# Turning the activations of two gated feed-forwards on VectorE instead of TensorE, in an fp32 two-layer block kernel

## The chip, the core and the metric

The kernel runs on one core of a Trainium2 chip, as one launch. The metric is the device time of the whole launch in microseconds (us), lower is better. Names of engines in the rows: PE is TensorE's matmuls, PEld its weight loads, DVE is VectorE, ACT is ScalarE, POOL is GpSimd, SP is SyncE, which here only issues DMAs.

## The reference, cut to what matters

Two transformer blocks over 256 tokens of width 1024, in fp32. The first has differential attention, retention and a squared-ReLU feed-forward; the second has, around its attention, two gated feed-forwards of hidden width 2816, with separate weights. These two are what the change touches:

```python
def swiglu(x, w_gate, w_up, w_down):
    return (jax.nn.silu(x @ w_gate) * (x @ w_up)) @ w_down
...
x = x + FFN_RES * swiglu(rms_norm_2(x, ffn1_norm[l]), ffn1_w_gate[l], ffn1_w_up[l], ffn1_w_down[l])
...
x = x + FFN_RES * swiglu(rms_norm_2(x, ffn2_norm[l]), ffn2_w_gate[l], ffn2_w_up[l], ffn2_w_down[l])
```

`w_gate` and `w_up` are 1024 x 2816, `w_down` is 2816 x 1024.

## The kernel before, in words

Every fp32 product is made of three products of a reduced type, fp32r: both operands are split into a high part (rounded) and a low part (what is left), and high x high, high x low and low x high are added up in PSUM. So each weight is streamed from HBM once, in **units** of 128 x 2048 (1 MB), in program order. For each unit SyncE issues the load into `raw`, one of 6 buffers; ScalarE writes the high part (`hi(u)`, line 1128, into `w_hi`, one of 4 buffers); VectorE writes the low part in place (`lo(u)`, line 1570, `w_lo<-raw,w_hi`); TensorE then uses both (`products`, line 523). `hi(u)` waits until TensorE has used unit u-4, the load until it has used unit u-6.

Activations need the same split, and must in addition lie with the contracted dimension on the partitions. A gated feed-forward (called a stage here: `f1` and `f2` in the names) is worked in 11 **blocks** of 256 hidden columns. For a block i:

- TensorE multiplies the normed tokens (`hA`) by the gate and up columns, two units of K, for two halves of 128 tokens each (`tb` 0 and 1): 2 x 2 x 4 x 3 = 48 matmuls of 128 x 512 (`ff_up`).
- ScalarE takes SiLU of the gate half (`silu`, line 1389, `act_r`), VectorE multiplies it by the up half (`multiply`, line 1906, `act_f<-bank,rs,act_r`). `act_f` has the tokens on the partitions.
- TensorE turns `act_f` with four 128 x 128 transposes (`ff_turn`, line 537, `bank<-masks,act_f`; `masks` holds the identity), two into each of the PSUM banks 6 and 7. ScalarE writes their high part (line 1135, `fT_hi<-bank`), VectorE the low part (line 1589, `fT_lo<-bank,fT_hi`), each in two instructions.
- TensorE multiplies `fT` by the block's 256 rows of `w_down`, one unit: 24 matmuls of 128 x 512 (`down`).

The work is pipelined by one block: **step i** of TensorE is the first 24 matmuls of `ff_up(i)`, the turn of block i-1, the other 24 matmuls of `ff_up(i)`, and `down(i-1)`. A step uses three units, v, v+1 (gate and up) and v+2 (down). VectorE's step i is `lo(v+3)`, the two low parts of block i-1, `lo(v+4)`, `multiply(i, 0)`, `multiply(i, 1)`, `lo(v+5)`; ScalarE's is `hi(v+3)`, the two high parts, `hi(v+4)`, two `silu`, `hi(v+5)`. Every engine runs its instructions in the written order. Steps 2 to 9 are a hardware loop of two rounds of four; step 1 and step 10 are written out. **Step 1** has in front of it, on VectorE, `multiply(0, 0)`, `multiply(0, 1)` and `lo(u+4)`. **Step 10** is written in another order: `up(0)` for tokens 0 to 127 with the turn of block 9 in its middle, then `up(1)` for tokens 128 to 255, with half of the turn of block 10 in its middle (two transposes, which wait for `multiply(10, 0)`), then the down products of block 9 and 10. On VectorE step 10 begins with the low parts of block 9, then `lo(v+3)`, then `multiply(10, 0)`.

Of the kernel before, what the change touches and what calls it, by code (L numbers as in the profile page):

```python
# [28 lines left out]
P = 128  # L29
D, TB, SEQ = 1024, 2, 256  # L30
# [5 lines left out]
HALF = 512  # L36
# [11 lines left out]
FF2 = 2816  # L48
SUB = 256
# [47 lines left out]
def work_batches():  # L97

    order = [("mix", 0, 0), ("mix", 1, 0), ("mix", 0, 1), ("mix", 1, 1)]
    for k in range(IN_CB):  # L100
        if k == 1:
            order += [("qk", 0, tb) for tb in range(TB)]
        if 6 <= k < 14:
            order += [("a", k - 6), ("v", k - 6)]
        if k == IN_CB - 1:
            order += [("ya", 0, 0)]
        if 12 <= k:
            order += [("rv", k - 12)]
    order += [("ya", 0, 1)]
    order += [("ya", 1, h) for h in range(2)]  # L110
    order += [("yr", tb, h) for tb in range(TB) for h in range(2)]
    order += [("m", tb, h) for tb in range(TB) for h in range(2)]
    order += [("mlp", tb, h) for tb in range(TB) for h in range(2)]
    order += [("p",)]
    order += [("ff", 0, tb) for tb in range(TB)]
    order += [("ple", tb, h) for tb in range(TB) for h in range(2)]
    order += [("ffn1", tb, h) for tb in range(TB) for h in range(2)]
    order += [("f1", i, tb) for i in range(FF2 // SUB) for tb in range(TB)]
    order += [("mix2", tb, h) for tb in range(TB) for h in range(2)]
    order += [("mq", tb) for tb in range(TB)] + [("cq", 0), ("cq", 1), ("ckv",)] + [("mk", tb) for tb in range(TB)]  # L120
    for kind in "bl":
        for j in range(BH // 2):
            order += [(kind + "a", 2 * j), (kind + "a", 2 * j + 1)]
            order += [(kind + "v", j)]
    order += [("ffn2", tb, h) for tb in range(TB) for h in range(2)]
    order += [("f2", i, tb) for i in range(FF2 // SUB) for tb in range(TB)]
    return {name: n for n, name in enumerate(order)}
# [38 lines left out]


# [17 lines left out]
def two_blocks(nc, x_d, p_d, g_mix, w_in, lam_q1, lam_k1, lam_q2, lam_k2, g_diff, g_ret, w_bd, w_br, w_out,  # L185
# [85 lines left out]
    fT, pT, fE = [fT0, fT1], [pT0, pT1], [fE0, fE1]  # L271
    (mix_t,) = lay(named["va"], ("mix_t", [P, TB, D]))
# [66 lines left out]
    f_hi, f_ready = sem("f_hi"), sem("f_ready")  # L339
    up_done, act_ready, up_out = sem("up_done"), sem("act_ready"), sem("up_out")  # L340
# [160 lines left out]
    def _(pe):  # L501
# [302 lines left out]
        def ff_up(u, name, i, steps, cols, du=0, di=0):  # L804

            for j in range(2):
# [7 lines left out]
                if j == 0:  # L814
                    ff_turn(name, i - 1, 2 * steps, cols, di)
# [94 lines left out]
        def gated(name, norm, base):  # L910
# [4 lines left out]

            def down(v, i, tb, r=0, first=False, last=False):

                turned((name, i, tb), 4 * r)
                return products([acc(tb, c)[:, :] for c in range(2)], fT, 2 * (i % 2), 2, tb, v, D, first, last,
                                12 * r)  # L920
# [11 lines left out]
            with pe.Fori(0, 2) as r:  # L932
# [5 lines left out]
            narrow_block(up(0)[:, :], None, v, 0, HALF, lambda: ff_turn(name, i - 1, 2 * (base + i), SUB))\  # L938
                .then_inc(up_done, 1)
# [8 lines left out]
            else:  # L948
                turned((name, i - 1, 1))
# [165 lines left out]
    def _(act):  # L1115
# [268 lines left out]
        def gated(name, norm, base):  # L1384
# [6 lines left out]

            silu(0, 0)
# [3 lines left out]
            def step(i, r=0):  # L1396
                v = u + 2 + 3 * (i - 1)
                hi(v + 3, r)
                for tb in range(TB):
                    split((name, i - 1, tb), 4 * r)  # L1400
# [9 lines left out]
            for tb in range(TB):  # L1410
                split((name, i - 1, tb))
# [143 lines left out]
    def _(vec):  # L1555
# [343 lines left out]
        def gated(name, norm_in, base, norm_out):  # L1899
# [8 lines left out]

            multiply(0, 0)
# [3 lines left out]
            def step(i, r=0):  # L1913
                v = u + 2 + 3 * (i - 1)
                lo(v + 3, 12 * r)
                for tb in range(TB):
                    split((name, i - 1, tb), 4 * r)
# [9 lines left out]
            for tb in range(TB):  # L1927
                split((name, i - 1, tb))
# [404 lines left out]
```

## Time and profile before

| | |
|---|---|
| median of 3 runs | 989.23 us (989.2, 989.23, 989.52) |
| profiled execution: span | 987.5 us |
| median less that span | 1.73 us (the page gives no other time for the profiled execution than its span) |
| TensorE busy | 980.2 us of the span |
| VectorE busy | 594.7 us |
| ScalarE busy | 499.4 us |
| first gated stage, first to last `act_f` instruction | 509.7 to 671.7 us |
| second gated stage | 807.6 to 973.3 us |

How to read the rows further down: a timeline row is start, length, engine, line, operation, the tile written, then the tiles read, and shapes; x2 says that two instructions were merged, and the length then reaches from the start of the first to the end of the second. A bracket says how long the engine had been idle before, and who released it. Matmuls overlap each other, so the time that one takes from the others is the distance between starts, not its length. A row for a group of instructions has its count, its busy time in us, and the mean length of one in ns.

### The profile page before, as it was taken

What the parts mean: (1) busy time and instruction counts of PE and PEld (TensorE: products, weight loads), DVE (VectorE), ACT (ScalarE), POOL (GpSimd) and SP (SyncE); (2) the same over time, 40 slices, a digit from 0 to 9 for tenths busy, and PEclk for the clock granted to TensorE, in tenths of its full rate; (3) what the DMA queues carried; (4) which work ended last, traced back from release to release, by engine and by line L of the source; (5) the groups of instructions that cost most, each with busy time, mean ns of one, the idle gap of its engine ahead of it and who ended that gap; (6) DMA issues with size and microseconds to landing.
All of it is one profiled execution on the core that took longest, in us unless ns stands there. A gap on an engine that the chain in (4) does not pass through costs nothing.

```text
span 987.5 us, 13371 instructions
## 1 busy us (share of the span) xinstructions
PE 980.2 (99%) x5000; PEld 822.2 (83%) x5000; DVE 594.7 (60%) x847; ACT 499.4 (51%) x707; POOL 65.6 (7%) x97
## 2 busy tenths in 40 slices
PE   9999999999999999999999999999999999999997
PEld 7989888888889888888888888888887788888886
DVE  6646655478666555665775545446758875455544
ACT  7444555744365444444684444435648664343433
POOL 4101000020020000000120000000203020000000
PEclk9999999999999999999999999999999999999999
DMA  9754554434465555544566555544654245555531
GB/s 345 253 177 165 171 171 161 154 129 171 171 224 198 197 187 188 196 179 168 180 213 200 184 184 199 174 145 134 218 174 147 86 172 196 187 180 202 171 127 43
DMA packets 98726, 175.71 MB, mean 178 GB/s; under 512 B 5920, under 2 KB 54128, under 8 KB 98672
## 3 DMA queue, kind: packets, MB, share of 16 engines
q1 hardware_dynamic: 97024, 171.53, 50.3%
q0 software_dynamic: 1344, 3.19, 1.2%
q8 instruction: 35, 0.57, 0.2%
q10 hardware_dynamic: 304, 0.27, 0.1%
q14 instruction: 19, 0.16, 0.1%
HBM read 173.91 MB, written 1.05 MB: 177 GB/s over the span
## 4 chain that ended last, share of the span: by engine, by line
PE 99%; issue 0%; DVE 0%; ACT 0%; POOL 0%; POOLq 0%; ACTq 0%
PE bank L523 76%; PE bank L644 6%; PE bank L857 5%; PE bank L537 4%; PE bank L859 2%; PE bank L836 1%; PE bank L582 1%; PE bank L581 1%; PE bank L593 1%; PE bank L991 1%; PE bank L678 0%; PE bank L1053 0%; PE bank L595 0%; PE bank L594 0%; PE bank L613 0%
## 5 line engine op out<-in xcount | busy, mean ns | idle before, releaser
L1570 DVE TENSOR_TENSOR w_lo<-raw,w_hi 128x2048 fp32r<-128x2048 f32 (+1 forms) x159 | 359.2, 2264 | 223.3 <-ACT w_hi L1128 223.2
L523 PE MATMUL bank<-w_hi,hA 128*128 128x512 f32 (+1 forms) x1368 | 431.6, 392 | 0.0
L1128 ACT ACTIVATE w_hi<-raw 128x2048 fp32r<-128x2048 f32 (+1 forms) x162 | 306.1, 1894 | 178.3 <-PE bank L523 133.2
L523 PEld LDWEIGHTS bank<-w_hi,hA 128*128 128x128 f32 x1368 | 255.4, 188 | 51.3 <-issue 0.6
L523 PE MATMUL bank<-w_lo,hA 128*128 128x512 f32 (+1 forms) x684 | 259.8, 387 | 0.0
L523 PEld LDWEIGHTS bank<-w_lo,hA 128*128 128x128 f32 x684 | 128.6, 188 | 25.0
L523 PE MATMUL bank<-w_hi,fT_hi 128*128 128x512 f32 x232 | 71.9, 391 | 0.0
L523 PE MATMUL bank<-w_lo,fT_hi 128*128 128x512 f32 x232 | 71.5, 390 | 0.0
L523 PE MATMUL bank<-w_hi,fT_lo 128*128 128x512 f32 x232 | 71.5, 389 | 0.0
L857 PE MATMUL bank<-hA,w_hi 128*128 128x512 f32 x192 | 68.0, 398 | 0.0
L1135 ACT ACTIVATE fT_hi<-bank 128x256 fp32r<-128x256 f32 (+1 forms) x46 | 15.9, 391 | 86.2 <-PE bank L537 86.2
L644 PE MATMUL bank<-hA,w_hi 128*128 128x256 f32 x320 | 58.2, 284 | 0.0
L859 PE MATMUL bank<-hA,w_lo 128*128 128x256 f32 x192 | 53.9, 281 | 0.0
L523 PEld LDWEIGHTS bank<-w_lo,fT_hi 128*128 128x128 f32 x232 | 43.6, 188 | 9.2
L523 PEld LDWEIGHTS bank<-w_hi,fT_lo 128*128 128x128 f32 x232 | 43.6, 188 | 9.1
L644 PEld LDWEIGHTS bank<-hA,w_hi 128*128 128x128 f32 x320 | 49.9, 192 | 0.5 <-ACT va L1180 0.3
L523 PEld LDWEIGHTS bank<-w_hi,fT_hi 128*128 128x128 f32 x232 | 43.0, 188 | 8.8 <-issue 0.2
L2187 POOL TENSOR_SCALAR ms<-ss 128x1 f32<-128x1 f32 x15 | 9.2, 615 | 609.8 <-ACT junk L1158 609.5
L1389 ACT ACTIVATE act_r<-bank,rs 128x256 f32<-128x256 f32 x44 | 20.9, 475 | 53.9 <-PE bank L523 52.2
L644 PE MATMUL bank<-hA,w_lo 128*128 128x256 f32 x160 | 45.3, 283 | 0.0
L1589 DVE TENSOR_TENSOR fT_lo<-bank,fT_hi 128x256 fp32r<-128x256 f32 (+1 forms) x46 | 18.1, 431 | 45.1 <-ACT fT_hi L1135 45.1
L857 PEld LDWEIGHTS bank<-hA,w_hi 128*128 128x128 f32 x192 | 36.1, 188 | 8.9
(306 smaller groups left out, 1086.6 us busy)
## 6 DMA issues: line engine op xcount, KB each, us to landing
raw<-in_w_in SPq DMA_DIRECT2D x74, 512.0 KB, 4.4
raw<-in_w_ff SPq DMA_DIRECT2D x64, 512.0 KB, 4.1
raw<-in_ffn_w_gate SPq DMA_DIRECT2D x44, 512.0 KB, 3.6
raw<-in_ffn_w_up SPq DMA_DIRECT2D x44, 512.0 KB, 4.5
raw<-in_ffn_w_down SPq DMA_DIRECT2D x44, 512.0 KB, 4.0
raw<-in_w_out SPq DMA_DIRECT2D x16, 512.0 KB, 4.1
raw<-in_w_branch_diff SPq DMA_DIRECT2D x8, 512.0 KB, 3.7
raw<-in_w_branch_ret SPq DMA_DIRECT2D x8, 512.0 KB, 4.2
```

The costliest lines, as they stand in the source:

```text
L523: mm = pe.matmul(o, a, w, start=first and t == 0 and m < len(outs), stop=last and t == n - 1 and m >= len(todo) - len(outs))
L537: mm = pe.transpose(work(name)[0:cols, col:col + rows], blk, ident)
L581: pe.matmul(b[:, 0:P], q[:, h, 0:P], k[:, h, 0:P], start=True, stop=True)
L582: pe.matmul(b[:, P:384], q[:, h, P:SEQ], k[:, h, :], start=True, stop=True).then_inc(score_done, 1)
L644: mm = pe.matmul(out, w, a[:, kt, :], start=(j, f % 2, t, m) == (0, 0, 0, 0), stop=(j, t, m) == (1, 3, 2), skip_group_check=True)
L857: pe.matmul(out[:, :], hi, hA_both[:, kt, :, :], start=(j, t) == (0, 0), stop=(j, t) == (1, 3), skip_group_check=True)
L859: mm = pe.matmul(out[:, 0:SEQ], lo, hA[0][:, kt, :], start=False, stop=(j, t) == (1, 3), skip_group_check=True)
L1128: act.activation(w_hi[u % HI_SLOTS][:, 0:w], raw[u % RAW_SLOTS][:, 0:w], ACT.Copy).then_inc(hi_ready, 1)
L1135: act.activation(dst, b, ACT.Copy).then_inc(split_hi, 1)
L1389: act.activation(act_r[:, tb, 0:SUB], up(tb, i)[:, 0:SUB], ACT.Silu, scale=inv_rms(norm, tb))\
L1570: vec.tensor_tensor(w_lo[u % RAW_SLOTS][:, 0:w], raw[u % RAW_SLOTS][:, 0:w], w_hi[u % HI_SLOTS][:, 0:w].bitcast(f32), ALU.subtract).then_i ...
L1589: vec.tensor_tensor(dst, b, hi.bitcast(f32), ALU.subtract).then_inc(work_out[WB[name] % 2], 1)
```

## The change

In blocks 0 to 9 of each gated stage (20 in all) TensorE's four transposes are left out. VectorE turns the block instead (`turn_act`): sixteen transposes of 32 partitions, each of which takes one quarter of the partitions of `act_f` (tokens) and moves 32 x 32 squares into one quarter of the partitions of a new SBUF buffer `act_T`, 128 elements for each partition. Of two in a row each writes another quarter of the partitions; after every four the quarter that is read changes too. ScalarE then writes the high part from `act_T` in one instruction of 128 x 512 (`turned_split`), VectorE the low part in one instruction of 128 x 512 (`turned_low`). TensorE waits for that low part at the head of `down`. Block 10 is turned by TensorE as before. PSUM banks 6 and 7 are no longer written in between, and the numbering of their users shrinks by 20 for each stage. Loads and weight splits stay as they were.

In the step, `turn_act(i-1)` is now the first thing on VectorE, ahead of `lo(v+3)`; the low part stays behind `lo(v+3)`.

```diff
--- before.py
+++ after.py
@@ -115,7 +115,7 @@
     order += [("ff", 0, tb) for tb in range(TB)]
     order += [("ple", tb, h) for tb in range(TB) for h in range(2)]
     order += [("ffn1", tb, h) for tb in range(TB) for h in range(2)]
-    order += [("f1", i, tb) for i in range(FF2 // SUB) for tb in range(TB)]
+    order += [("f1", FF2 // SUB - 1, tb) for tb in range(TB)]
     order += [("mix2", tb, h) for tb in range(TB) for h in range(2)]
     order += [("mq", tb) for tb in range(TB)] + [("cq", 0), ("cq", 1), ("ckv",)] + [("mk", tb) for tb in range(TB)]
     for kind in "bl":
@@ -123,7 +123,7 @@
             order += [(kind + "a", 2 * j), (kind + "a", 2 * j + 1)]
             order += [(kind + "v", j)]
     order += [("ffn2", tb, h) for tb in range(TB) for h in range(2)]
-    order += [("f2", i, tb) for i in range(FF2 // SUB) for tb in range(TB)]
+    order += [("f2", FF2 // SUB - 1, tb) for tb in range(TB)]
     return {name: n for n, name in enumerate(order)}
 
 
@@ -164,6 +164,8 @@
         SPLIT[_name] = _n
         _n += 1
 
+
+TURNED = {"f1": 0, "f2": FF2 // SUB - 1}
 
 TALL = (1, 2, 3, 6, 7)
 
@@ -269,6 +271,7 @@
         ("pT_hi", [P, 2, SEQ], f32r), ("pT_lo", [P, 2, SEQ], f32r), ("p_sb", [P, TB, 256]), ("gain_mid", [P, D]),
         ("fE_hi", [P, 4, SEQ], f32r), ("fE_lo", [P, 4, SEQ], f32r))
     fT, pT, fE = [fT0, fT1], [pT0, pT1], [fE0, fE1]
+    (act_T,) = lay(named["fE_lo"] + 16 * SEQ, ("act_T", [P, 2, SEQ]))
     (mix_t,) = lay(named["va"], ("mix_t", [P, TB, D]))
 
     (mq_tm, mk_tm, mv, mqT, mkT, cq, ckv, q_tm, k_tm, v_tm, qT, kT, pos_k, posdist, kr) = lay(
@@ -337,6 +340,7 @@
     ones_ready, diag_ready, row_done, row_ready = (sem(n) for n in ("ones_ready", "diag_ready", "row_done", "row_ready"))
     acc_done, acc_out = sem("acc_done"), sem("acc_out")
     f_hi, f_ready = sem("f_hi"), sem("f_ready")
+    act_turned, turned_hi, turned_lo = sem("act_turned"), sem("turned_hi"), sem("turned_lo")
     up_done, act_ready, up_out = sem("up_done"), sem("act_ready"), sem("up_out")
     score_done, score_out = sem("score_done"), sem("score_out")
     bias_ready = sem("bias_ready")
@@ -811,8 +815,6 @@
                     if j and tb == 0:
                         mm.then_inc(up_done, 1)
                 mm.then_inc(unit_used, 1)
-                if j == 0:
-                    ff_turn(name, i - 1, 2 * steps, cols, di)
 
 
         u = U0["ff"]
@@ -913,9 +915,14 @@
             u, n = U0[name], FF2 // SUB
             ff_up0(u, norm)
 
+            t0 = TURNED[name]
+
             def down(v, i, tb, r=0, first=False, last=False):
 
-                turned((name, i, tb), 4 * r)
+                if i == n - 1:
+                    turned((name, i, tb))
+                else:
+                    pe.wait_ge(turned_lo, t0 + i + 1 + 4 * r)
                 return products([acc(tb, c)[:, :] for c in range(2)], fT, 2 * (i % 2), 2, tb, v, D, first, last,
                                 12 * r)
 
@@ -935,8 +942,7 @@
 
             v, i = u + 2 + 3 * (n - 2), n - 1
             pe.wait_ge(up_out, 2 * (base + i))
-            narrow_block(up(0)[:, :], None, v, 0, HALF, lambda: ff_turn(name, i - 1, 2 * (base + i), SUB))\
-                .then_inc(up_done, 1)
+            narrow_block(up(0)[:, :], None, v, 0, HALF).then_inc(up_done, 1)
             narrow_block(up(1)[:, :], None, v, 1, HALF, lambda: ff_turn(name, i, 2 * (base + n), SUB, blocks=(0,)))
             down(v + 2, i - 1, 0)
             ff_turn(name, i, 2 * (base + n), SUB, blocks=(1,))
@@ -946,7 +952,7 @@
                 src_turn("mix2", 0)
                 down(v + 3, i, 1, last=True).then_inc(unit_used, 1)
             else:
-                turned((name, i - 1, 1))
+                pe.wait_ge(turned_lo, t0 + i)
                 turned((name, i, 1))
                 pe.wait_ge(lo_ready, v + 4)
                 for c0, c1 in LAST:
@@ -1389,6 +1395,10 @@
                 act.activation(act_r[:, tb, 0:SUB], up(tb, i)[:, 0:SUB], ACT.Silu, scale=inv_rms(norm, tb))\
                    .then_inc(act_ready, 1)
 
+            def turned_split(i, r=0):
+                act.wait_ge(act_turned, TURNED[name] + i + 1 + 4 * r)
+                act.activation(fT[0][:, 2 * (i % 2):2 * (i % 2) + 2, :], act_T[:, :, :], ACT.Copy).then_inc(turned_hi, 1)
+
             silu(0, 0)
             silu(0, 1)
             hi(u + 4)
@@ -1396,8 +1406,7 @@
             def step(i, r=0):
                 v = u + 2 + 3 * (i - 1)
                 hi(v + 3, r)
-                for tb in range(TB):
-                    split((name, i - 1, tb), 4 * r)
+                turned_split(i - 1, r)
                 hi(v + 4, r)
                 for tb in range(TB):
                     silu(i, tb, r)
@@ -1407,8 +1416,7 @@
                 for i in range(2, 6):
                     step(i, r)
             v, i = u + 2 + 3 * (n - 2), n - 1
-            for tb in range(TB):
-                split((name, i - 1, tb))
+            turned_split(i - 1)
             hi(v + 3)
             silu(i, 0)
             split((name, i, 0))
@@ -1906,15 +1914,31 @@
                 vec.scalar_tensor_tensor(out=act_f[:, tb, 0:SUB], in0=up(tb, i)[:, SUB:2 * SUB], scalar=rs[:, n:n + 1],
                                          in1=act_r[:, tb, 0:SUB], op0=ALU.mult, op1=ALU.mult).then_inc(up_out, 1)
 
+            def turn_act(i, r=0):
+
+                vec.wait_ge(up_out, 2 * (base + i) + 2 + 8 * r)
+                whole = act_f[:, :, 0:SUB].rearrange("p t (k j f) -> p t k j f", j=4, f=32)
+                there = act_T[:, :, :].rearrange("p k (t a c) -> p t k a c", a=4, c=32)
+                for a in range(4):
+                    for j in range(4):
+                        t = vec.transpose(there[32 * j:32 * j + 32, :, :, a, :], whole[32 * a:32 * a + 32, :, :, j, :])
+                t.then_inc(act_turned, 1)
+
+            def turned_low(i, r=0):
+
+                vec.wait_ge(turned_hi, TURNED[name] + i + 1 + 4 * r)
+                hi, dst = (t[:, 2 * (i % 2):2 * (i % 2) + 2, :] for t in fT)
+                vec.tensor_tensor(dst, act_T[:, :, :], hi.bitcast(f32), ALU.subtract).then_inc(turned_lo, 1)
+
             multiply(0, 0)
             multiply(0, 1)
             lo(u + 4)
 
             def step(i, r=0):
                 v = u + 2 + 3 * (i - 1)
+                turn_act(i - 1, r)
                 lo(v + 3, 12 * r)
-                for tb in range(TB):
-                    split((name, i - 1, tb), 4 * r)
+                turned_low(i - 1, r)
                 lo(v + 4, 12 * r)
                 for tb in range(TB):
                     multiply(i, tb, r)
@@ -1924,8 +1948,8 @@
                 for i in range(2, 6):
                     step(i, r)
             v, i = u + 2 + 3 * (n - 2), n - 1
-            for tb in range(TB):
-                split((name, i - 1, tb))
+            turn_act(i - 1)
+            turned_low(i - 1)
             lo(v + 3)
             multiply(i, 0)
             split((name, i, 0))
```

How the instructions stand. **VectorE, head of the first gated stage** (the end of the work ahead of the loop; `act_f` is written by the multiplies of block 0, `fT_lo` is the low part that `down(0)` waits for). Before:

```order
L1906 SCALAR_TENSOR_TENSOR act_f<-bank,rs,act_r 128x256 x2
L1570 TENSOR_TENSOR w_lo_77<-raw_71,w_hi_83 128x2048
L1570 TENSOR_TENSOR w_lo_78<-raw_72,w_hi_84 128x2048
L1589 TENSOR_TENSOR fT_lo<-bank,fT_hi 128x2x128 x2
L1570 TENSOR_TENSOR w_lo_79<-raw_73,w_hi_85 128x2048
```

With the change:

```order
L1914 SCALAR_TENSOR_TENSOR act_f<-bank,rs,act_r 128x256 x2
L1578 TENSOR_TENSOR w_lo_77<-raw_71,w_hi_83 128x2048
L1924 STREAM_TRANSPOSE act_T<-act_f 32x2x2x32 x16
L1578 TENSOR_TENSOR w_lo_78<-raw_72,w_hi_84 128x2048
L1931 TENSOR_TENSOR fT_lo<-act_T,fT_hi 128x512
```

Sixteen instructions have come in between the same two weight splits, ahead of the low part.

**VectorE, step 10 of the first gated stage** (behind the loop; the second row of `act_f` is not shown). Before:

```order
L1589 TENSOR_TENSOR fT_lo<-bank,fT_hi 128x2x128 x2
L1570 TENSOR_TENSOR w_lo_81<-raw_75,w_hi_83 128x2048
L1906 SCALAR_TENSOR_TENSOR act_f<-bank,rs,act_r 128x256
L1589 TENSOR_TENSOR fT_lo<-bank,fT_hi 128x2x128
L1570 TENSOR_TENSOR w_lo_76<-raw_70,w_hi_84 128x1536
```

With the change:

```order
L1924 STREAM_TRANSPOSE act_T<-act_f 32x2x2x32 x16
L1931 TENSOR_TENSOR fT_lo<-act_T,fT_hi 128x512
L1578 TENSOR_TENSOR w_lo_81<-raw_75,w_hi_83 128x2048
L1914 SCALAR_TENSOR_TENSOR act_f<-bank,rs,act_r 128x256
L1597 TENSOR_TENSOR fT_lo<-bank,fT_hi 128x2x128
```

Here nothing stands between the transposes and the low part, and the weight split and the multiply of block 10 stand behind both.

**TensorE, step 1 of the first gated stage**, between the two units of `ff_up(1)`. Before:

```order
L523 MATMUL bank<-w_lo_81,hA 128x512
L523 MATMUL bank<-w_hi_85,hA 128x512
L537 MATMUL bank<-masks,act_f 128x128 x4
L523 MATMUL bank<-w_hi_82,hA 128x512
L523 MATMUL bank<-w_lo_76,hA 128x512
```

With the change:

```order
L527 MATMUL bank<-w_lo_81,hA 128x512
L527 MATMUL bank<-w_hi_85,hA 128x512
L527 MATMUL bank<-w_hi_82,hA 128x512
L527 MATMUL bank<-w_lo_76,hA 128x512
L527 MATMUL bank<-w_hi_82,hA 128x512 x2
```

The four transposes are gone, and nothing else has moved on this engine.

## Rows read from the trace of the kernel before

**Rows 1.** The page: busy time of each engine, and TensorE's granted clock over the span.
```profile
PE 980.2 (99%) x5000; PEld 822.2 (83%) x5000; DVE 594.7 (60%) x847; ACT 499.4 (51%) x707; POOL 65.6 (7%) x97
...
PEclk9999999999999999999999999999999999999999
```

**Rows 2.** The page: the chain that ended last, shares by engine.
```profile
PE 99%; issue 0%; DVE 0%; ACT 0%; POOL 0%; POOLq 0%; ACTq 0%
```

**Rows 3.** Timeline of TensorE over one step in the first gated stage.
```profile
573.25 0.39 PE L523 MATMUL bank<-w_hi,hA 128*128 128x512 f32 x1
...
578.70 0.60 PE L537 MATMUL bank<-masks,act_f 128*128 128x128 f32 x4
...
584.62 0.62 PE L523 MATMUL bank<-w_hi,fT_hi 128*128 128x512 f32 x2
...
590.07 0.39 PE L523 MATMUL bank<-w_hi,hA 128*128 128x512 f32 x1
```

**Rows 4.** Groups of VectorE and ScalarE by shape, whole span.
```profile
L1570 DVE TENSOR_TENSOR w_lo<-raw,w_hi 128x2048 fp32r<-128x2048 f32 x153 | 350.4, 2295 | 221.4 <-ACT w_hi L1128 221.3
...
L2065 DVE COPY aT<-bank 128x384 f32<-128x384 f32 x8 | 4.4, 553 | 0.0
...
L1844 DVE TENSOR_TENSOR fT_lo<-act_f,fT_hi 128x512 fp32r<-128x512 f32 x6 | 3.9, 684 | 0.0
...
L2050 DVE COPY yT<-bank 128x256 f32<-128x256 f32 x8 | 3.3, 419 | 0.8 <-PE bank L992 0.8
...
L1320 ACT ACTIVATE fT_hi<-act_f 128x512 fp32r<-128x512 f32 x6 | 3.5, 632 | 0.0
```

**Rows 5.** Timeline of VectorE: short instructions in a row.
```profile
685.46 2.16 DVE L1597 SCALAR_TENSOR_TENSOR hA<-bank,g_col,hA 128x128 fp32r<-128x128 f32 x8 [2.98 <-ACT hA L1140]
...
692.99 0.18 DVE L2002 TENSOR_SCALAR turns__163<-ang 128x32 f32<-128x32 f32 x1
693.20 0.38 DVE L2003 TENSOR_SCALAR turns__163<-turns__163 128x32 f32<-128x32 f32 x1
```

**Rows 6.** Timeline of VectorE over a step in the first gated stage.
```profile
570.32 2.29 DVE L1570 TENSOR_TENSOR w_lo<-raw,w_hi 128x2048 fp32r<-128x2048 f32 x1 [1.32 <-ACT w_hi L1128]
575.48 2.29 DVE L1570 TENSOR_TENSOR w_lo<-raw,w_hi 128x2048 fp32r<-128x2048 f32 x1 [2.86 <-ACT w_hi L1128]
579.53 0.76 DVE L1589 TENSOR_TENSOR fT_lo<-bank,fT_hi 128x256 fp32r<-128x256 f32 x2 [1.76 <-ACT fT_hi L1135]
```

**Rows 7.** Timelines of VectorE and TensorE, step 1 of the first gated stage.
```profile
512.24 4.49 DVE L1570 TENSOR_TENSOR w_lo<-raw,w_hi 128x2048 fp32r<-128x2048 f32 x2 [1.32 <-ACT w_hi L1128]
516.65 0.74 DVE L1589 TENSOR_TENSOR fT_lo<-bank,fT_hi 128x256 fp32r<-128x256 f32 x2
...
517.37 0.66 PE L523 MATMUL bank<-w_hi,fT_hi 128*128 128x512 f32 x2
```

**Rows 8.** Timelines of VectorE and TensorE, step 1 of the second gated stage.
```profile
810.55 4.49 DVE L1570 TENSOR_TENSOR w_lo<-raw,w_hi 128x2048 fp32r<-128x2048 f32 x2 [1.32 <-ACT w_hi L1128]
...
819.02 0.62 PE L523 MATMUL bank<-w_hi,fT_hi 128*128 128x512 f32 x2
```

**Rows 9.** Timelines of VectorE, ScalarE and TensorE, step 10 of the first gated stage.
```profile
654.35 2.29 DVE L1570 TENSOR_TENSOR w_lo<-raw,w_hi 128x2048 fp32r<-128x2048 f32 x1 [1.32 <-ACT w_hi L1128]
...
660.96 1.92 ACT L1128 ACTIVATE w_hi<-raw 128x2048 fp32r<-128x2048 f32 x1
...
665.12 0.48 DVE L1906 SCALAR_TENSOR_TENSOR act_f<-bank,rs,act_r 128x256 f32<-128x256 f32 x1
...
665.92 0.38 PE L537 MATMUL bank<-masks,act_f 128*128 128x128 f32 x2
```

**Rows 10.** Last matmul, then stretches behind it: engines' busy us, TensorE's clock, DMA share, GB/s.
```profile
981.66 0.28 PE L958 MATMUL bank<-w_hi,fT_lo 128*128 128x256 f32 x1
...
982.00:984.50 2.50, 0.00 (x0) 0.00 (x0) 1.58 (x5) 1.10 (x3) 0.55 (x1) 1.00 0.52 213
984.50:985.00 0.50, 0.00 (x0) 0.00 (x0) 0.00 (x0) 0.03 (x1) 0.00 (x0) 0.74 0.00 0
985.00:987.00 2.00, 0.00 (x0) 0.00 (x0) 0.00 (x0) 0.00 (x0) 0.00 (x0) 0.50 0.68 262
```

## The prediction, made before the changed kernel ran

> **What bounds the kernel now.** I read the page first. TensorE is busy for 980.2 of 987.5 us, its granted clock is at the top level in every slice [rows 1], and the chain that ended last runs through TensorE for 99% of its length [rows 2]. VectorE and ScalarE have 40% and 49% of the span free. So whatever is taken off TensorE comes off the time, provided that nobody makes it wait; and every wait that is added to it is paid in full, since no slack follows in which it could be made up. The question is therefore not whether VectorE has the time on average. It is when its results are due. For that I went to the timelines of one middle step, and then to the first and last step of each gated stage.
>
> A change of 0.2%, 2 us, is about what a measurement of this kernel can tell from none.
>
> **What is removed.** In a middle step [rows 3], 24 matmuls stand between 573.25 and 578.70 us (5.45 us) and 24 more between 584.62 and 590.07 us (5.45 us). Between 578.70 and 584.62 us stand the four transposes and 24 matmuls: 5.92 us. The transposes with their change of type thus cost 5.92 - 5.45 = 0.47 us for a block. Twenty blocks: **-9.4 us**. The PSUM reads that go (two on ScalarE, two on VectorE for each block) were on engines that idled, and give nothing.
>
> **What one new transpose costs.** The trace has no transpose on VectorE. Its instructions from one source have a fixed and a growing part: a copy of 256 elements takes 419 ns, one of 384 takes 553 [rows 4], so 134 ns for 128 elements, and 128 elements would take 419 - 134 = 285 ns. What counts is the distance from start to start. For instructions that overlap it is less than the length: eight of 128 elements take 2.16 us together, some 260 ns each [rows 5]. For instructions that wait for the one before it is more: one of 0.18 us is followed after 0.21 us [rows 5]. The sixteen have no wait between them, but each writes another group of 32 partitions than the one before, which no instruction of this trace does. The low end is 0.20 us (285 less the 85 ns by which a `w_lo` of 2.29 us overlaps the next one, two of them in 4.49 us, [rows 7]). The high end is four times the growing part, 285 + 3 x 134 = 690 ns, were a turned element to cost four. I take 0.32 us, the 285 ns with the 30 ns of a serial pair: it is nearest to a copy of this size, and I see no row that shows overlap across groups of partitions. Sixteen: 5.1 us for a block.
>
> The overlapping rows and the Trainium skill differ here. The page "VectorE: DVE Perf Modes", section "Two Vector instructions with no wait between them", says that an instruction whose output starts in another quarter of the partitions than the last output is held until all earlier ones have finished. By the overlap of the rows the sum below would end at a gain, by the rule near or above zero; no run here shows it yet.
>
> **A middle step hides it.** VectorE is done with the previous step at 572.61 and idles 2.86 us until ScalarE hands it the next unit [rows 6]. The transposes start in that gap and end at 577.7. Then `lo(v+3)` (2.21 from start to start) until 579.9 and the low part, 128 x 512, 0.68 us [rows 4], until 580.6. It is due when `down` starts, 584.62 less 0.47, so 3.5 us are left over. ScalarE's high part (0.63 us, [rows 4]) fits beside `lo(v+3)`, and its `hi(v+4)`, which waits for TensorE at 578.70 anyway, starts no later. VectorE's sum for a step is 3 x 2.21 + 0.68 + 2 x 0.48 + 5.1 = 13.4 us of TensorE's 16.35 (16.82 less 0.47). So eight middle steps of each stage wait for nothing. That cover ends where one transpose passes about 0.5 us.
>
> **Step 1 does not hide it.** In the first stage VectorE runs two weight splits back to back from 512.24 and the two low parts end at 517.39, which is when `down(0)` starts: 517.37 [rows 7]. There is no slack at all. Now the first split passes on at 514.45, the transposes end at 519.57, `lo(v+3)` passes on at 521.78, the low part ends at 522.46, and TensorE sees it some 0.05 us later, at 522.5. It gets there at 517.37 - 0.47 = 516.9. **A wait of 5.6 us.** Behind it VectorE does `lo(v+4)`, the multiplies and `lo(v+5)` beside the 5.4 us of `down(0)`, so step 2 starts in order.
>
> The second stage has more air. The split passes on at 812.75 [rows 8]; 5.12 + 2.21 + 0.68 + 0.05 later it is 820.8, against 819.02 - 0.47 = 818.55. **A wait of 2.3 us.**
>
> **Step 10 does not hide it either.** Its order puts the low part straight behind the transposes and `hi(v+3)` of ScalarE behind the high part. VectorE is free at 656.64 [rows 9]; transposes until 661.76; ScalarE's high part until 662.4 and `hi(v+3)` until 664.25 (1.92 us, overlapping by 0.1); `lo(v+3)` until 666.57, `multiply(10, 0)` until 667.0. TensorE wants it for the half turn of block 10 at 665.92 - 0.47 = 665.45 [rows 9]. **A wait of 1.6 us in each stage**, 3.1 together. The second stage has the same distances.
>
> **The clock.** Behind its last matmul TensorE idles, and the granted clock is still full until 984.5 and at half (1.2 GHz) from 985 [rows 10]: it was full for the first 2.5 us without a matmul and low after 3. A wait of 5.6 us is longer than that, one of 2.3 us shorter. So I expect the clock to be low when `down(0)` of the first stage starts. No row shows how it comes back under work. The ends are nothing and 5.4 us, all of `down(0)` at half speed; I take **1.4 us**, nearer to nothing, because every slice under work, the first one too, is at the full clock [rows 1].
>
> **The sum.** -9.4 + 5.6 + 2.3 + 3.1 + 1.4 = **+3.0 us**. The span of the profiled execution would go from 987.5 to 990.5; the median of the runs lies 1.73 us above that span, and I add the same 3.0 to it: 989.23 + 3.0 = **992.2 us**.
>
> With T the distance between two transposes, the four waits are 0.5 + 16T, 16T - 2.9, and twice 16T - 3.6 (each nothing below zero). So one more hundredth of a microsecond in T costs 0.64 us, and the change breaks even, clock aside, at T = 0.297.
>
> **The rivals.**
>
> *Overlap, and a gain.* The sixteen run like the eight of [rows 5] or closer, at 0.26 down to 0.20 us. At 0.235 (16T = 3.8) the waits are 4.3, 0.9 and twice 0.2, 5.6 in all: 5.6 - 9.4 = -3.8, so 985.4 us, with the clock's 1.4 us 986.8; at 0.20 it is 983.8. For it speak the rows of every other pair without a wait; against it that none of them changes the group of partitions. It decides from T below 0.297 on; by the page's rule it would not happen.
>
> *Dearer transposes, still hidden in the middle.* If filling and emptying a 32 x 32 square isn't hidden, or 4-byte elements go at less than one per cycle, T is 0.36 to 0.5. At 0.42 the waits are 0.5 + 6.7, 3.8 and twice 3.1, 17.2 in all, and with the clock +9.2: 998.4 us. No row speaks for it or against it.
>
> *VectorE becomes the bound.* At T = 0.69 a step of VectorE takes 8.3 + 11.0 = 19.3 us against 16.8 before. Sixteen middle steps: +40 us; the waits at the ends are 34 us by the same formulas: about 1060 us. Against it: a growing part of four times that of a copy.
>
> *The change does not do what it says.* TensorE might not get faster, if the 0.47 us belonged to something else than the transposes. Against it: the same step with and without them differs in nothing else. The waits alone would make it 1001.6 us.
>
> **How the numbers follow.** Forecast, T from 0.29 to 0.35 with or without the clock: 0.55; its own range is 988.8 (0.29, clock kept) to 994.0 (0.35, with the clock's 1.4 us). Overlap: 0.2. Dearer, hidden: 0.17. VectorE bound: 0.05. No saving: 0.03. The range reaches from 985.5, in the middle of the overlap case, to 1001.0, T about 0.46; beyond lie some 0.1 of overlap and some 0.1 of the others. Faster by over 0.2% (below 987.3) is most of the overlap case: 0.2. Slower by over 0.2% (above 991.2) is 0.3 of the forecast's 0.55 and all the dear cases: 0.55. Within 0.2%: 0.25.
>
> **What the profile after would show.** The 80 transposes of TensorE gone and a middle step of 16.35 us; VectorE's transposes 0.3 us apart, starting each as the last ends; `fT_lo` in a middle step more than 3 us ahead of its use; TensorE idle once for 5.6 us near 517, once for 2.3 near 810, and twice for 1.6 in the steps 10; a granted clock below full in one slice near 520. The prediction is wrong if the transposes overlap (waits then shrink by 16 times the difference in T), if a middle step has a wait, or if TensorE's idle time at step 1 is short because VectorE was sooner free than in the rows.

## The result and the profile after

The changed kernel takes 993.52 us (median of 4 runs, 993.26 to 995.31), the kernel before 989.31 us beside it (4 runs, 989.2 to 989.52). The ratio is 1.0044, with a 95% interval of 1.0032 to 1.0057: slower by 0.4%. The profiled execution took 993.32 us with a span of 991.4 us, 3.9 us more than the span before. I forecast +3.0.

The page of the changed kernel, against [rows 1] and [rows 2]: busy time of each engine, TensorE's granted clock in 40 slices, and the engines' shares of the chain that ended last.

```profile
PE 973.7 (98%) x4920; PEld 815.9 (82%) x4920; DVE 687.0 (69%) x1147; ACT 500.4 (50%) x687; POOL 65.9 (7%) x97
...
PEclk9999999999999999999998999999999999999999
...
PE 91%; DVE 4%; ACT 2%; issue 1%; POOL 1%; POOLq 0%; ACTq 0%; DVEq 0%
```

TensorE's work did shrink, by 80 instructions and 6.5 us of busy time. VectorE grew by 92 us and is still free for 31% of the span. Yet VectorE and ScalarE now have 6% of the chain, where they had nothing. The slice below full clock is the one with 521 us in it.

The waits of TensorE in the changed kernel (bank, line and what was waited for: us in all, times, longest):

```profile
PE bank L527 <- DVE fT_lo L1931: 7.9, 2, 5.6
PE bank L541 <- DVE act_f L1914: 2.5, 2, 1.2
PE bank L682 <- DVE junk L1679: 1.5, 1, 1.5
```

The third row lies at the very start of the kernel (TensorE idles until 1.46 us), stands in the kernel before as well, and is not of this change. The first two are all four of the waits that were forecast, and there is no other: 16 of the 20 steps wait for nothing.

VectorE in step 1 of the first stage, against [rows 7]:

```profile
511.89 2.29 DVE L1578 TENSOR_TENSOR w_lo<-raw,w_hi 128x2048 fp32r<-128x2048 f32 x1 [1.32 <-ACT w_hi L1134]
514.10 5.04 DVE L1924 STREAM_TRANSPOSE act_T<-act_f 32x128 f32<-32x128 f32 x16
519.17 2.29 DVE L1578 TENSOR_TENSOR w_lo<-raw,w_hi 128x2048 fp32r<-128x2048 f32 x1
521.38 0.68 DVE L1931 TENSOR_TENSOR fT_lo<-act_T,fT_hi 128x512 fp32r<-128x512 f32 x1
```

Sixteen transposes fill 5.04 us. The median one is 303 ns long, so from start to start it is (5.04 - 0.30) / 15 = 0.316 us, and the block passes VectorE on after 5.07 us.

TensorE in both stages, against [rows 3], [rows 7], [rows 8] and [rows 9]:

```profile
516.30 0.39 PE L527 MATMUL bank<-w_hi,hA 128*128 128x512 f32 x1
522.33 1.19 PE L527 MATMUL bank<-w_hi,fT_hi 128*128 128x512 f32 x2 [5.64 <-DVE fT_lo L1931]
...
530.33 0.39 PE L527 MATMUL bank<-w_hi,hA 128*128 128x512 f32 x1
...
546.64 0.39 PE L527 MATMUL bank<-w_hi,hA 128*128 128x512 f32 x1
...
557.52 0.61 PE L527 MATMUL bank<-w_hi,fT_hi 128*128 128x512 f32 x2
...
562.97 0.39 PE L527 MATMUL bank<-w_hi,hA 128*128 128x512 f32 x1
...
668.82 0.39 PE L527 MATMUL bank<-w_hi,hA 128*128 128x512 f32 x1
670.45 0.44 PE L541 MATMUL bank<-masks,act_f 128*128 128x128 f32 x2 [1.25 <-DVE act_f L1914]
...
822.88 0.39 PE L527 MATMUL bank<-w_hi,hA 128*128 128x512 f32 x1
825.55 0.70 PE L527 MATMUL bank<-w_hi,fT_hi 128*128 128x512 f32 x2 [2.29 <-DVE fT_lo L1931]
```

A matmul of this stream gives way to the next after 0.23 us (24 in 5.45 us, [rows 3]). So what a wait costs is the time to the next start less 0.23: in step 1 of the first stage 522.33 - 516.53 = 5.80 us, in that of the second 825.55 - 823.11 = 2.44, in step 10 of the first 670.45 - 669.05 = 1.40, and as much in that of the second. The middle step is 562.97 - 546.64 = 16.33 us, 0.49 less than the 16.82 before. And `down(0)` of the first stage takes 530.33 - 522.33 = 8.0 us for the 24 matmuls that take 5.45 in a middle step (557.52 to 562.97).

Why it does is in the stretches of the changed kernel (stretch, length, busy us of PE, PEld, DVE, ACT and POOL, granted clock, DMA share, GB/s):

```profile
518.00:520.00 2.00, 0.00 (x0) 0.00 (x0) 1.93 (x5) 0.82 (x2) 0.00 (x0) 1.00 0.86 241
520.00:522.00 2.00, 0.00 (x0) 0.00 (x0) 2.00 (x3) 2.00 (x3) 0.00 (x0) 0.69 0.79 279
522.00:526.00 4.00, 3.67 (x9) 2.93 (x10) 4.00 (x5) 2.13 (x2) 0.00 (x0) 0.50 0.00 0
526.00:527.50 1.50, 1.50 (x5) 1.20 (x4) 1.49 (x3) 0.00 (x0) 0.00 (x0) 0.50 0.00 0
527.50:530.00 2.50, 2.50 (x12) 2.01 (x11) 2.40 (x8) 0.00 (x0) 0.00 (x0) 0.98 0.00 0
```

The clock is still at 2.4 GHz until about 520.7 us, 4 us into the wait, falls to its lower level (1.2 GHz) while TensorE still waits, and comes back to 2.4 GHz after some 5.2 us of matmuls, half of which are lost: 8.00 - 5.45 = 2.55 us.

The account of the span: 5.80 + 2.44 + 2 x 1.40 + 2.55 = 13.6 us lost, 20 x 0.49 = 9.8 gained, +3.8 of the +3.9 measured.

The other two places on VectorE and ScalarE. The middle step (against [rows 6]):

```profile
545.93 5.04 DVE L1924 STREAM_TRANSPOSE act_T<-act_f 32x128 f32<-32x128 f32 x16
551.00 2.29 DVE L1578 TENSOR_TENSOR w_lo<-raw,w_hi 128x2048 fp32r<-128x2048 f32 x1
553.21 0.68 DVE L1931 TENSOR_TENSOR fT_lo<-act_T,fT_hi 128x512 fp32r<-128x512 f32 x1
```

The low part is ready at 553.89 and used at 557.52: 3.6 us to spare. Step 10 (against [rows 9]):

```profile
660.16 5.04 DVE L1924 STREAM_TRANSPOSE act_T<-act_f 32x128 f32<-32x128 f32 x16
...
665.24 0.63 ACT L1400 ACTIVATE fT_hi<-act_T 128x512 fp32r<-128x512 f32 x1 [7.32 <-DVE act_T L1924]
...
665.78 1.90 ACT L1134 ACTIVATE w_hi<-raw 128x2048 fp32r<-128x2048 f32 x1
...
667.71 2.29 DVE L1578 TENSOR_TENSOR w_lo<-raw,w_hi 128x2048 fp32r<-128x2048 f32 x1 [1.11 <-ACT w_hi L1134]
...
669.92 0.48 DVE L1914 SCALAR_TENSOR_TENSOR act_f<-bank,rs,act_r 128x256 f32<-128x256 f32 x1
```

One thing ends as the next begins: transposes, high part, `hi(v+3)`, `lo(v+3)`, `multiply(10, 0)`, and 0.05 us behind it TensorE's half turn at 670.45. ScalarE idled for 7.32 us, ready to do `hi(v+3)`, because that stood behind a high part that waited for the transposes.

### The profile page after: what moved, and what is told of

Its sections match the earlier page's. It is cut to its first block, busy times and chain, and to the rows that moved or that the text cites. A ratio compares the mean times of both kernels' runs of the same rounds, so it can differ in the third digit from the quotient of the medians.

```text
span 991.4 us, 13423 instructions
## 1 busy us (share of the span) xinstructions
PE 973.7 (98%) x4920; PEld 815.9 (82%) x4920; DVE 687.0 (69%) x1147; ACT 500.4 (50%) x687; POOL 65.9 (7%) x97
## 4 chain that ended last, share of the span: by engine, by line
PE 91%; DVE 4%; ACT 2%; issue 1%; POOL 1%; POOLq 0%; ACTq 0%; DVEq 0%
PE bank L527 69%; PE bank L648 6%; PE bank L859 5%; PE bank L541 3%; PE bank L861 2%; DVE act_T L1924 2%; DVE w_lo L1578 1%; ACT w_hi L1134 1%; PE bank L838 1%; PE bank L586 1%; PE bank L585 1%; PE bank L597 1%; PE bank L997 1%; POOL ms L2211 0%; POOL rs L2212 0%
## 5 line engine op out<-in xcount | busy, mean ns | idle before, releaser
L527 PE MATMUL bank<-w_hi,hA 128*128 128x512 f32 (+1 forms) x1368 | 426.0, 390 | 0.0
L1924 DVE STREAM_TRANSPOSE act_T<-act_f 32x128 f32<-32x128 f32 x320 | 96.7, 302 | 4.1
L1400 ACT ACTIVATE fT_hi<-act_T 128x512 fp32r<-128x512 f32 x20 | 12.6, 632 | 58.7 <-DVE act_T L1924 58.7
```

Source lines behind the costliest of these rows:

```text
L527: mm = pe.matmul(o, a, w, start=first and t == 0 and m < len(outs), stop=last and t == n - 1 and m >= len(todo) - len(outs))
L1400: act.activation(fT[0][:, 2 * (i % 2):2 * (i % 2) + 2, :], act_T[:, :, :], ACT.Copy).then_inc(turned_hi, 1)
L1924: t = vec.transpose(there[32 * j:32 * j + 32, :, :, a, :], whole[32 * a:32 * a + 32, :, :, j, :])
```

## The experiments

The theory that these rows give: each block saves TensorE 0.49 us; the middle steps hide the rest; steps 1 and 10 don't; and the sixteen transposes are as long as they are because each is held until the one before has ended. The rivals are those of the prediction. All times stand beside runs of the kernel before on the same chip (989.4 to 989.5 us).

**Taking back one end at a time.** In the first experiment block 0 of both stages is turned by TensorE again, with its four PSUM reads; the rest is as in the changed kernel.

```diff
+ON_PE = (0,)
...
 def step(i, r=0):
     v = u + 2 + 3 * (i - 1)
-    turn_act(i - 1, r)
+    if i - 1 not in ON_PE:
+        turn_act(i - 1, r)
     lo(v + 3, 12 * r)
-    turned_low(i - 1, r)
+    if i - 1 in ON_PE:
+        for tb in range(TB):
+            split((name, i - 1, tb))
+    else:
+        turned_low(i - 1, r)
```

> Block 0 of both stages is turned by TensorE again, blocks 1 to 9 stay on VectorE. Theory (four waits at the ends of the stages, one of which drops the clock, against 0.47 us gained for each block): the waits of 5.6 and 2.3 us in the steps 1 and the 2.6 us of the low clock go, two blocks of 0.47 us come back: 993.4 - 10.5 + 0.9 = 983.8 us. Rival (the middle steps give back the gain, VectorE being busier throughout): the time stays above 987.

Measured: 983.54 us (983.48 to 983.75), ratio 0.994 [0.9926, 0.9953]. Two blocks of twenty, given back, turn a loss of 4.2 us into a gain of 5.9. TensorE's waits left in the two stages:

```profile
PE bank L549 <- DVE act_f L1935: 2.5, 2, 1.2
```

The two kernels are 10.0 us apart, and the two blocks given back cost 1.0 us. So the two waits at step 1 and the clock are worth 11.0 us, against 5.80 + 2.44 + 2.55 = 10.8 us in the trace of the changed kernel.

In the second it is block 9 (`ON_PE = (9,)`, the same edit in step 10).

> Block 9 of both stages is turned by TensorE again. Theory: only the two waits of 1.6 us in the steps 10 go, two blocks of 0.47 us come back: 993.4 - 3.2 + 0.9 = 991.1 us, with the wait of 5.6 us and the low clock near 520 us still there. Rival (the order of step 10 does not matter): 993.4 + 0.9 = 994.3 us.

Measured: 991.15 us (7 runs, 990.58 to 993.5), ratio 1.0024 [1.0012, 1.0035]. The waits on `act_f` are gone, those on `fT_lo` are as in the changed kernel:

```profile
PE bank L535 <- DVE fT_lo L1952: 7.9, 2, 5.6
```

Five runs lie at 990.6 to 991.6, where the theory has it, and two at 993.4 and 993.5 with a mean clock 0.002 to 0.003 lower. I come back to that under the hardware.

With both, `ON_PE = (0, 9)`:

> Blocks 0 and 9 are turned by TensorE, 1 to 8 by VectorE. Theory: no wait is left, 16 blocks of 0.47 us are gained: 989.3 - 7.5 = 981.8 us, some 0.9 us above e5. Rival (a middle step gives less than 0.47 us): above 983.

Measured: 981.79 us (981.12 to 982.59), ratio 0.9924 [0.991, 0.9937]. The two ends add up, and sixteen blocks on VectorE gain 7.7 us, 0.48 each.

**The clock by itself.** 44 matmuls of 128 x 256, whose result nobody uses, stand in TensorE's wait at step 1 of the first stage. They do nothing else than keep it busy.

```diff
     pe.wait_ge(up_out, 2 * base + 2)
+    if tb == 0 and name == "f1":
+        for _ in range(44):
+            pe.matmul(bank[7][:, 0:SEQ], hA[0][:, 0, 0:P], hA[0][:, 0, :], start=True, stop=True)
 mm = down(v + 2, i - 1, tb, r, i == 1)
```

> In step 1 of the first stage TensorE fills its wait with 44 extra matmuls of 128 x 256 into an unused bank, some 5.1 us; the wait itself stays. Theory (the low clock is a second price of the same wait): the granted clock stays full and down(0) takes 5.4 us instead of 8.0: 993.4 - 2.6 = 990.8 us. Rival (down(0) is slow for another reason, such as VectorE and ScalarE at work on SBUF beside it): 993.4 us.

Measured: 991.86 us (11 runs, 990.97 to 992.58), ratio 1.0023 [1.0014, 1.0032]. TensorE's timeline of this kernel, and a stretch of it in the columns as before:

```profile
517.38 0.39 PE L535 MATMUL bank<-w_hi,hA 128*128 128x512 f32 x1
517.60 5.43 PE L946 MATMUL bank<-hA 128*128 128x256 f32 x44
523.21 0.73 PE L535 MATMUL bank<-w_hi,fT_hi 128*128 128x512 f32 x2 [0.18 <-DVE fT_lo L1955]
...
528.81 0.39 PE L535 MATMUL bank<-w_hi,hA 128*128 128x512 f32 x1
...
524.00:526.00 2.00, 2.00 (x10) 1.64 (x9) 2.00 (x3) 1.24 (x1) 0.00 (x0) 1.00 0.00 0
```

The wait is as long, 5.6 us from 517.60 to 523.21, but `down(0)` now takes 5.6 us instead of 8.0 at full clock. The low clock is therefore a cost of its own on top of the wait. In this trace the distance from the last matmul ahead of the wait to the next step is 528.81 - 517.38 = 11.43 us, against 530.33 - 516.30 = 14.03 in the changed kernel: 2.6 us less, as expected. The profiled run as a whole is only 1.5 us shorter, because it came to the stage 1.1 us later (517.38 against 516.30), ahead of anything that the edit touches. Five of the runs, at 990.97 to 991.11, give the 2.5 us back in full; five, at 992.36 to 992.58, only 1.0, with a mean clock 0.002 to 0.003 lower.

**Are the transposes held?** Here the sixteen write the quarter of the partitions that they read, four in a row the same one. What is left out is the moving of squares from one quarter to another; number, length and bytes stay.

```diff
-t = vec.transpose(there[32 * j:32 * j + 32, :, :, a, :], whole[32 * a:32 * a + 32, :, :, j, :])
+t = vec.transpose(there[32 * a:32 * a + 32, :, :, j, :], whole[32 * a:32 * a + 32, :, :, j, :])
```

> The sixteen transposes keep their count and size, but four in a row read and write one and the same quarter of the partitions (the squares are not moved between quarters, so block contents are turned only within a quarter). Theory (each waits for the one before only because the quarter changes): distance from start to start falls from 0.316 us to about 0.23 for 12 of 16, the block takes 3.9 us instead of 5.04, the four waits shrink by 1.1 us each: 988.8 us with the low clock, 986.2 without it. Rival (a transpose never overlaps the next one): distance 0.316 us as before, 993.4 us.

Measured: 987.15 us (10 runs, 986.76 to 988.23), ratio 0.998 [0.997, 0.9989]. VectorE's block, TensorE's waits at step 1, and the first of them with the start of the next step, in this kernel:

```profile
514.50 3.57 DVE L1945 STREAM_TRANSPOSE act_T<-act_f 32x128 f32<-32x128 f32 x16
...
PE bank L535 <- DVE fT_lo L1952: 5.0, 2, 4.2
...
521.26 0.79 PE L535 MATMUL bank<-w_hi,fT_hi 128*128 128x512 f32 x2 [4.17 <-DVE fT_lo L1952]
```

The block takes 3.57 us instead of 5.04 (3.9 was expected), so 1.47 us are the price of changing quarters: for three in four of these instructions the quarter does not change. The single instructions say the same. In this kernel two of the same quarter start 0.19 to 0.24 us apart, while at the three changes of quarter the distance is 0.27 us, and there the next starts 0.01 us after the last has ended. A rival is that an instruction is slow because it moves its squares to another quarter, whatever stands before it; this experiment took that away too. The changed kernel's own trace speaks against it: four of its sixteen write the quarter that they read, and they are as long (0.29 to 0.31 us) and as far apart (0.31 to 0.32 us) as the others. Each wait on the low part is shorter by 1.5 us, those in step 10 are gone, and the kernel is faster than before by 2.3 us: the overlap rival, whose condition does not hold in the real change.

Does the read side or the written side hold them? With the loops exchanged, three in four write the same quarter as the last and read another one. (This experiment, and the two with extra transposes further down, are edits of the best version, the one at 980.76 us.)

```diff
-for a in range(4):
-    for j in range(4):
+for j in range(4):
+    for a in range(4):
         t = vec.transpose(there[32 * j:32 * j + 32, :, :, a, :], whole[32 * a:32 * a + 32, :, :, j, :])
```

> As e5, with the two loops over quarters swapped: four transposes in a row write the same quarter and read another one each. Theory A (a change of quarter on either side holds the next instruction): distance 0.316 us as before, 5.04 us for a block. Theory B (only a change on the written side holds it): 12 of 16 overlap, 3.6 us for a block as in e6. The time is 980.8 us under both, since nobody waits for the transposes.

Measured, in one execution: 980.68 us beside 989.44, and the block in it:

```profile
538.41 5.05 DVE L1941 STREAM_TRANSPOSE act_T<-act_f 32x128 f32<-32x128 f32 x16
```

It is as long as in the written order. Either side holds. Any two of the sixteen differ in the quarter that they read or in the one that they write, so no order of them escapes it. The Trainium skill says this of both sides ("VectorE: DVE Perf Modes", section "Two Vector instructions with no wait between them"); the three orders here agree with it (5.04, 5.05, and 3.57 where neither changes).

**The best version.** Block 0 on TensorE, and step 10 in the order of a middle step: ScalarE's `hi(v+3)` ahead of the turned high part, VectorE's `lo(v+3)` between the transposes and the low part.

```diff
+ON_PE = (0,)
...
-turned_split(i - 1)
 hi(v + 3)
+turned_split(i - 1)
...
 turn_act(i - 1)
-turned_low(i - 1)
 lo(v + 3)
+turned_low(i - 1)
 multiply(i, 0)
```

> As e1 (block 0 back on TensorE), and in step 10 both orders are those of the middle steps: ScalarE hi(v+3) ahead of the high part of block 9, VectorE lo(v+3) between the transposes and the low part. Theory (the wait of step 10 comes from its order alone): multiply(10, 0) ends 7.75 us after the step's start and is due at 8.17, no wait is left on TensorE in either stage: 983.5 - 2.9 = 980.6 us, and that is the gain of 18 blocks of 0.47 us over the kernel before (989.3 - 8.5 = 980.8). Rival (it is the transposes' length): some 1.5 us of wait stay in each step 10, 983.5 us.

Measured: 980.76 us (980.66 to 981.07), ratio 0.9913 [0.99, 0.9927], 8.7 us below the kernel before. Step 10 of the first stage in it, VectorE and TensorE, and TensorE's only wait of over 0.2 us in the whole span, the one at the start of the kernel:

```profile
652.65 5.05 DVE L1941 STREAM_TRANSPOSE act_T<-act_f 32x128 f32<-32x128 f32 x16
657.73 2.29 DVE L1595 TENSOR_TENSOR w_lo<-raw,w_hi 128x2048 fp32r<-128x2048 f32 x1
659.94 0.68 DVE L1948 TENSOR_TENSOR fT_lo<-act_T,fT_hi 128x512 fp32r<-128x512 f32 x1
660.54 0.48 DVE L1931 SCALAR_TENSOR_TENSOR act_f<-bank,rs,act_r 128x256 f32<-128x256 f32 x1
...
661.53 0.38 PE L549 MATMUL bank<-masks,act_f 128*128 128x128 f32 x2
...
PE bank L690 <- DVE junk L1696: 1.5, 1, 1.5
```

The weight split now covers the hand-over to ScalarE, and `multiply(10, 0)` is done 0.5 us before TensorE wants it. Eighteen blocks gain 18 x 0.49 = 8.8 us, and that is what is measured.

**How much cover do the middle steps have?** On that version, eight and then sixteen more transposes of each block, into a buffer that nobody reads.

```diff
+more = more_T[:, :, :].rearrange("p k (t a c) -> p t k a c", a=4, c=32)
+for n in range(8):
+    a, j = n // 4, n % 4
+    t = vec.transpose(more[32 * j:32 * j + 32, :, :, a, :], whole[32 * a:32 * a + 32, :, :, j, :])
 t.then_inc(act_turned, 1)
```

> As e5, with 8 transposes more for each block that VectorE turns, into a buffer that nobody reads, in front of its signal: 7.6 us for a block instead of 5.04. Theory (slack of 3.5 us in a middle step): the middle steps still hide it, low part ready at 9.8 us of the step and due at 10.9, so they keep 16.35 us; only step 10 waits, 2.1 us in each stage: 980.6 + 4.3 = 984.9 us. Rival (VectorE's load makes the middle steps longer before it is full): 16 middle steps longer by some tenths of a us each, above 988.

Measured: 987.0 us (7 runs, 985.22 to 988.87), ratio 0.9976 [0.9965, 0.9987]. Two middle steps, the wait in step 10, and two stretches behind it, in the profiled run of this kernel (988.24 us):

```profile
571.90 0.39 PE L536 MATMUL bank<-w_hi,hA 128*128 128x512 f32 x1
...
588.22 0.39 PE L536 MATMUL bank<-w_hi,hA 128*128 128x512 f32 x1
...
663.72 0.44 PE L550 MATMUL bank<-masks,act_f 128*128 128x128 f32 x2 [1.90 <-DVE act_f L1932]
...
664.00:666.00 2.00, 2.00 (x9) 1.64 (x8) 0.44 (x2) 1.76 (x2) 0.00 (x0) 0.73 0.49 171
666.00:668.00 2.00, 2.00 (x6) 1.54 (x6) 1.75 (x1) 0.00 (x0) 0.00 (x0) 0.50 0.00 0
```

The step is 16.32 us: 2.5 us more on VectorE cost the middle nothing. The waits in step 10 are the expected ones, 1.9 us. What was not expected is the clock behind them. By the stretches it falls at about 664.9 us, when TensorE has been at work again for 1.2 us, and is back at about 668.3 (0.92 over 668 to 670 us): 3.4 us at the lower level, 1.7 us lost. The second stage shows the same once more, 0.57 and 0.58 over 965 to 967 and 967 to 969 us. Two times 1.7 us lost is what the profiled run lies above the expectation (988.24 against 984.9). The median lies 2.1 us above it; the fastest run, at 985.22, is where no low clock would put it, so that the clock fell in some stages of some runs and not in others is likely, but only one run has a trace.

> As e7, with 16 transposes more for each block: 10.1 us for a block. Theory: a step of VectorE is 8.3 + 10.1 = 18.4 us against 16.35 of TensorE, the step becomes 18.4 us and VectorE the bound in the stages: about 980.6 + 43 = 1024 us. Rival (part of VectorE's sum overlaps): below 1000.

Measured: 1024.0 us (1022.33 to 1024.67), ratio 1.0352 [1.0336, 1.0368]. One step of TensorE, and its waits:

```profile
571.68 0.73 PE L536 MATMUL bank<-w_hi,fT_hi 128*128 128x512 f32 x2 [1.51 <-DVE fT_lo L1953]
...
589.81 0.73 PE L536 MATMUL bank<-w_hi,fT_hi 128*128 128x512 f32 x2 [1.53 <-DVE fT_lo L1953]
...
PE bank L536 <- DVE fT_lo L1953: 24.5, 16, 1.8
PE bank L550 <- DVE act_f L1932: 9.1, 2, 4.6
```

The step is 18.13 us (18.4 was expected): the cover is used up and VectorE sets the pace, 16 times. It ends between 24 and 32 transposes of 0.316 us, that is between 7.6 and 10.1 us of turning per block. An estimate from this step: VectorE needs 18.13 - 10.1 = 8.0 us for the rest of its work, so a step of 16.33 us has room for 8.3 us of turning. This is the rival in which VectorE becomes the bound, made by hand.

## Why the prediction was right

- **What is removed.** -9.4 us was forecast, 20 x 0.49 = -9.8 measured. The price was right because it was taken as a distance in the stream, with and without the transposes, and not as their busy time of 0.60 us. The rival in which nothing is saved is out.
- **One transpose.** T was taken as 0.32 us and is 0.316. The working put a length (285 ns) and the 30 ns of a serial pair together. The median length is 303 ns and the pair costs about 13 ns, so the two errors cancel. What decided it was not the size but whether instructions overlap. The rows of the kernel before could not show that; the experiment in which the quarters stay the same does. Between 3.57 and 5.04 us for a block lies the whole difference between a faster and a slower kernel.
- **The four waits.** Forecast 5.6, 2.3, 1.6 and 1.6 us, measured 5.8, 2.4, 1.4 and 1.4, at the four places. Taking block 0 back makes the first pair go, taking block 9 back the second.
- **The middle.** Forecast 16.35 us and 3.5 us to spare, measured 16.33 and 3.6. The cover was said to end at T of about 0.5, 8 us of turning for a block; 7.6 us were still hidden, 10.1 not, and the estimate above gives 8.3.
- **The clock** is the term that was mis-sized: 1.4 us taken between 0 and 5.4, 2.55 measured. I took the side near nothing because every slice under work was at the full clock. But that was a trace in which TensorE waited only once, for 1.5 us at the start, so it could not say how long the clock stays low under work. The middle of the bounds, 2.7, would have been nearer, though no row spoke for it. The comparison of the waits with the 2.5 to 3 us of [rows 10] named the right wait here, but it is no rule: in the changed kernel the clock was still full some 4 us into the wait, and with eight extra transposes it fell behind a wait of 1.9 us.
- **How the 1.3 us between 992.2 and 993.5 come about.** The clock is +1.2. The other terms together are -0.4: -0.4 for what is removed, +0.2 and +0.1 for the waits in the steps 1, -0.3 for those in the steps 10. The remaining +0.5 is in no term: 0.1 us of the span that the account leaves open, 0.2 because the time of the profiled execution stands 1.9 us above its span and not 1.73, and 0.2 because the median lies above the profiled execution. That the total came so close is in part luck.

The length of one instruction says little about such a choice. For the full turn of a block, two halves of 128 x 256 in fp32, TensorE needed four instructions and 0.49 us of its stream, VectorE sixteen instructions and 5.04 us. The Trainium skill's page "VectorE: DVE Perf Modes", section "The three transpose paths", gives 390 ns on TensorE and 311 ns on VectorE for 128 x 128 in bf16, and says that VectorE's turns only blocks of 32 x 32, each by itself. No run here has a bf16 transpose; that VectorE needs many instructions for a full turn is what this kernel shows.

## What to carry to other kernels

Work that goes from the bounding engine to an idle one is hidden where its result has slack, so look at the first and last step of a pipelined loop and not at the engine's share of idle time: here 16 of 20 blocks gained 7.7 us, and the four at the ends turned that into a loss of 4.2. Leave the first block on the old engine, give the last step the order of a middle one, and the same change gains 8.7 us. And price short VectorE instructions by where they start: 16 across quarters of the partitions took 5.04 us, 16 that kept to a quarter four at a time 3.57.

## What the runs showed of the hardware that was not expected

- TensorE's clock fell to 1.2 GHz behind a wait of 1.90 us in one kernel (eight extra transposes), 1.2 us after the matmuls had begun again, while in the profiled run of the changed kernel it stayed at 2.4 GHz after a wait of 2.29 us. Equal waits need not have equal prices.
- How long the clock stays low differs too. Behind the wait of 5.8 us it was low for 5.2 us of matmuls, which cost 2.55 us. Where the wait before was 4.2 us (squares that stay in their quarter) the clock was still full when the matmuls began again at 521.26 us and fell about 0.5 us later (0.93 over 520 to 522 us, 0.72 over 524 to 526): 3.4 us low, and `down(0)` took 7.12 us, 1.7 more than at full clock. Each of the two low stretches behind the waits of 1.9 us also was 3.4 us long.
- Some kernels spread more from run to run than others. With a wait of the change of 1.9 us or more the runs of one kernel spread over 1.5 to 3.7 us, and in two of them (block 9 back, and the filled wait) they fall into two groups 2.4 and 1.5 us apart, the longer with a mean clock 0.002 to 0.003 lower. But the kernel with blocks 0 and 9 back, in which no wait of the change is left, also spreads over 1.5 us (981.12 to 982.59), and 23 runs of the kernel before over 1.3 us (988.98 to 990.24), so a spread alone does not show a fallen clock. One wait whose clock falls in some executions and not in others would make such groups. Only one execution of each kernel has a trace, so which wait it is stays open, and so does whether the 995.31 us among the runs of the changed kernel is the same.
